# A third ring bank in PSUM, with the stick-breaking totals moved into a spent score bank

## The chip, the cores and the metric

The kernel runs on one core of one Trainium2 chip. The metric is device microseconds from the start to the end of one launch. Five engines work side by side and meet only at semaphores: TensorE (PE: matmuls, its weight loads are shown as PEld), VectorE (DVE), ScalarE (ACT), GpSimd (POOL) and SyncE (SP, which issues most DMAs). PE writes to PSUM alone, which has eight banks of 128 partitions x 512 float32 columns. All eight are in use here.

## The reference, cut to what matters

Two layers of a hybrid decoder. Each normalises x, projects it once for three branches (retention, stick-breaking attention, a conformer convolution), gates each branch, and projects the result back. What the change touches is the stick-breaking attention:

```
z = jnp.einsum('bqhd,bkhd->bhqk', qb, kb).astype(jnp.float32) * scale + bf
log_stop = jnp.where(mask, jax.nn.log_sigmoid(-z), 0.0)
after = lax.cumsum(log_stop, axis=3, reverse=True) - log_stop
A = jnp.where(mask, jnp.exp(jax.nn.log_sigmoid(z) + after), 0.0)
outs.append(jnp.einsum('bhqk,bkhd->bqhd', A.astype(v.dtype), vb))
```

The sum over later keys runs over all keys, so a kernel that goes through the keys block by block has to carry, for each query, the total of `log_stop` of the block that it has just done: what was gathered before is scaled by `exp(-total)`.

## The kernel before

1024 prompt tokens and 32 sampled ones stand as 1056 columns, in three chunks of 352 (`CH`, `CW`). A layer goes over three pairs of heads, p = 0, 1, 2. The order of all work is one list, `STEPS`, made once; every engine walks the same list and does its own part of each step, in that order, so an engine's queue is in the order of the list.

**Ring jobs.** Projections (`proj`: 24 matmuls for a chunk, in two float32r parts each, L691 to L693), rotations (`rot`), value transposes (`vtok`), the retention's steps (`att`, `ro`, `ds9`) and the norms' means and variances (`gn_...`, `ln_...`, `pw`) each write one PSUM bank of a ring of two, in turn. A job is drained by ACT or DVE. `claim` makes PE wait, ahead of a job, until the job two before it has been drained:

```
if jobs[job] >= 2:
    pe.wait_ge(*drained(in_order[jobs[job] - 2]))
```

**Stick-breaking units.** Twelve units a pair (`UNITS`): a key block `kb` against 128 to 512 queries, and two heads (h = 0, 1). Unit u has two score banks, Z[2(u%2)] and Z[2(u%2)+1]. Its steps:

- `score` (p, u): PE writes the scores into the two banks (L801, and a mask at L807). ACT takes exp (L962) into `stop`, POOL clamps it (L1484).
- ACT takes ln (L970) in step `weigh` (u-1), and DVE finishes the softplus (L1168).
- `stop` (p, u): PE adds the running sums to the scores in the banks (L814). ACT takes exp (L1122), the weights: the score bank's content is then spent. For every unit with kb > 0 (ten of twelve) PE also sums `stop` over the keys into a bank of its own, TOT (L822), for both heads, and ACT makes `keep` = exp(-total) from it (L1127).
- `weigh` (p, u): PE multiplies the weights with the values into the bank AV (L836). DVE multiplies what was gathered before by `keep` (L1380) and adds AV (L1382).

The list stands as score 0, then for each u: score u+1, stop u, weigh u. Between these the function `between` places ring jobs as filler, by fixed weights. In the first stretch of pair 1 DVE also does the convolution's taps (L1279, L1280).

The eight banks: ring0, ring1, Z0 to Z3, TOT, AV.

Of the kernel before, what the change touches and what calls it, by code (L numbers as in the profile page):

```python
# [247 lines left out]
def build(nc, io, counts):  # L248
# [4 lines left out]
    with ctx:  # L253
# [64 lines left out]
        old_x = attend[:, 0:KB * NT].rearrange("p (k n) -> p k n", k=KB)  # L318
        glu9 = sb("glu9", [P, CB, DEC_BATCH, HIST + DEC_SEQ])

        ring = [bank("ring0"), bank("ring1")]
        Z = [bank(f"Z{i}") for i in range(4)]
        TOT, AV = bank("TOT"), bank("AV")

        SUM_X, SUM_Y = [z[:, 0:CW] for z in Z[:3]], [z[:, 0:CW] for z in (Z[3], TOT, AV)]

        def cc(a, n=P):
            return const[:, a:a + n]
# [16 lines left out]
        U, B = len(UNITS), len(BLOCKS)  # L345

        z9 = Z[0][:, 0:6 * NS]

        def of_head(a, h):

# [160 lines left out]
        in_order = list(jobs)  # L511

        def in_ring(job):
            return ring[jobs[job] % 2][:, 0:CW]

        def bank_of(job):
            return ring[jobs[job] % 2]


        def scores_of(p, n, w):  # L520
# [147 lines left out]
        def _(pe):  # L668
            def claim(job):

                if jobs[job] >= 2:
                    pe.wait_ge(*drained(in_order[jobs[job] - 2]))

            for step in STEPS:
                kind = step[0]
# [25 lines left out]
                elif kind == "vtok":  # L701
# [3 lines left out]
                        pe.wait_ge(s_copy.sem, s_copy.at(job_of(name, p, CH - 1)))  # L705
                    for n in range(3 * j, 3 * j + 3):
                        t0 = n * P if n < QB else LAST
                        last = nc.tensor.transpose(ring[jobs[step] % 2][:, (n - 3 * j) * P:(n - 3 * j + 1) * P],
                                                   v_rows[:, t0:t0 + P], ident)
                    last.then_inc(s_full.sem, s_full.mark(step))  # L710
                elif kind == "att":
# [74 lines left out]
                elif kind == "score":  # L786
# [5 lines left out]
                    elif u == 0:  # L792
# [4 lines left out]
                            pe.wait_ge(s_masks, 16)  # L797
                        pe.wait_ge(s_copy.sem, s_copy.at(job_of("sk", p, CH - 1)))
                    for h in range(2):
                        r = slice(64 * h, 64 * h + 64)  # L800
                        last = nc.tensor.matmul(Z[2 * (u % 2) + h][:, 0:n], sb_k[r, kb * P:(kb + 1) * P], sb_q[r, q0:q0 + n],  # L801
                                                start=True, stop=not diagonal, skip_group_check=True)
                        if not diagonal:
                            last.then_inc(s_z.sem, s_z.mark((p, u, h)))
# [4 lines left out]
                elif kind == "stop":  # L809
                    p, u = step[1:]  # L810
                    kb, q0, n = UNITS[u]
                    for h in range(2):
                        pe.wait_ge(s_sp.sem, s_sp.at((p, u, h)))
                        nc.tensor.matmul(Z[2 * (u % 2) + h][:, 0:n], negtri, stop[:, (2 * u + h) % 4, 0:n], start=False,  # L814
                                         stop=True, skip_group_check=True).then_inc(s_za.sem, s_za.mark((p, u, h)))
                    if kb > 0:
                        if UNITS[u - 1][0] > 0:
                            pe.wait_ge(s_keepf.sem, s_keepf.at((p, u - 1)))
                        elif p > 0:
                            pe.wait_ge(s_keepf.sem, s_keepf.at((p - 1, U - 1)))  # L820
                        for h in range(2):
                            last = nc.tensor.matmul(TOT[64 * h:64 * h + 64, 0:n], ones[:, 0:64], stop[:, (2 * u + h) % 4, 0:n],  # L822
                                                    start=True, stop=True, skip_group_check=True)
                        last.then_inc(s_tot.sem, s_tot.mark((p, u)))
                elif kind == "weigh":
                    p, u = step[1:]
                    kb, q0, n = UNITS[u]
                    if u == 0:
                        pe.wait_ge(s_copy.sem, s_copy.at(("vtok", "sv", p, CH - 1)))
                        if p > 0:  # L830
                            pe.wait_ge(s_o.sem, s_o.at((p - 1, "sample")))
                    else:
                        pe.wait_ge(s_o.sem, s_o.at((p, u - 1)))
                    for h in range(2):
                        pe.wait_ge(s_a.sem, s_a.at((p, u, h)))
                        last = nc.tensor.matmul(AV[64 * h:64 * h + 64, 0:n], sb_v[:, kb, 64 * h:64 * h + 64],  # L836
                                                weight[:, h, 0:n], start=True, stop=True, skip_group_check=True)
                    last.then_inc(s_av.sem, s_av.mark((p, u)))
                elif kind == "sample_z":
                    p = step[1]  # L840
                    w = 2 * NS
                    zs = z9.rearrange("p (g b n) -> p g b n", g=3, b=DEC_BATCH)
                    q9 = q9_pad[:].rearrange("p h (b t) -> p b h t", b=DEC_BATCH)
                    pe.wait_ge(s_a.sem, s_a.at((p, U - 1, 1)))
                    pe.wait_ge(s_pagek.sem, s_pagek.at(p))
                    nc.tensor.matmul(z9[:, 2 * w:3 * w], sb_k[:, LAST:NT], q9, start=True, stop=False, skip_group_check=True)
                    nc.tensor.matmul(z9[:, 2 * w:3 * w], ident_b[:], masks[:, P:P + w], start=False, stop=False, skip_group_check=True)
                    for b in range(DEC_BATCH):
                        for g in range(N_PAGES):
                            last = nc.tensor.matmul(zs[:, g, b], page[:, b * N_PAGES + g, :], q9[:, b], start=False,  # L850
                                                    stop=False, skip_group_check=True)
                    last.then_inc(s_z.sem, s_z.mark((p, "sample")))
                elif kind == "sample_t":
                    p = step[1]
                    w = 2 * NS
                    pe.wait_ge(s_sp.sem, s_sp.at((p, "sample")))
                    s9 = stop9[:].rearrange("p g n -> p (g n)")

                    nc.tensor.matmul(z9, negtri, s9, start=False, stop=False, skip_group_check=True)
                    nc.tensor.matmul(z9[:, 0:2 * w], negones, s9[:, w:3 * w], start=False, stop=False, skip_group_check=True)  # L860
                    nc.tensor.matmul(z9[:, 0:w], negones, s9[:, 2 * w:3 * w], start=False, stop=True,
                                     skip_group_check=True).then_inc(s_za.sem, s_za.mark((p, "sample")))
                elif kind == "sample_v":
                    p = step[1]
                    w = 2 * NS
                    pe.wait_ge(s_a.sem, s_a.at((p, "sample")))
                    pe.wait_ge(s_pagev.sem, s_pagev.at(p))
                    pe.wait_ge(s_o.sem, s_o.at((p, U - 1)))
                    nc.tensor.matmul(AV[:, 0:w], sb_v[:, QB, :], weight9[:, 2, :], start=True, stop=False, skip_group_check=True)
                    for b in range(DEC_BATCH):  # L870
                        for g in range(N_PAGES):
                            q = slice(b * 2 * DEC_SEQ, (b + 1) * 2 * DEC_SEQ)
                            last = nc.tensor.matmul(AV[:, q], page[:, b * N_PAGES + g, :], weight9[:, g, q],
                                                    start=False, stop=(b == DEC_BATCH - 1 and g == N_PAGES - 1), skip_group_check=True)
                    last.then_inc(s_av.sem, s_av.mark((p, "sample")))
                elif kind == "sum_x":
                    c = step[1]
                    for k in range(KB):
                        pe.wait_ge(s_sqa.sem, s_sqa.at(("x", c, k)))
                        nc.tensor.matmul(SUM_X[c], ones, square_of_x(c, k), start=(k == 0), stop=(k == KB - 1)).then_inc(  # L880
                            s_sqm.sem, s_sqm.mark((c, k)))

        @block.scalar
        def _(act):
# [88 lines left out]
            for step in STEPS:  # L973
# [79 lines left out]
                elif kind == "vtok":  # L1053
                    _, name, p, j = step
                    if p > 0 and j == 0:
                        if name == "rv":
                            act.wait_ge(s_ds.sem, s_ds.at((p - 1, QB, 1)))
                        else:
# [1 line left out]
                    to = ret_v if name == "rv" else sb_v  # L1060
                    act.wait_ge(s_full.sem, s_full.at(step))
                    nc.scalar.activation(to[:, 3 * j:3 * j + 3, :],
                                         ring[jobs[step] % 2][:, 0:3 * P].rearrange("p (n e) -> p n e", n=3),
                                         ACT.Copy).then_inc(s_copy.sem, s_copy.mark(step))
                elif kind == "att":
                    p, n = step[1:]
# [46 lines left out]
                elif kind == "stop":  # L1113
# [6 lines left out]
                    for h in range(2):  # L1120
                        act.wait_ge(s_za.sem, s_za.at((p, u, h)))
                        nc.scalar.activation(weight[:, h, 0:n], Z[2 * (u % 2) + h][:, 0:n], ACT.Exp,  # L1122
                                             bias=vv(V_BIAS + 2 * p + h)).then_inc(s_a.sem, s_a.mark((p, u, h)))
                    if kb > 0:
                        act.wait_ge(s_tot.sem, s_tot.at((p, u)))
                        act.wait_ge(s_o.sem, s_o.at((p, u - 1)))
                        nc.scalar.activation(keep[:, 0:n], TOT[:, 0:n], ACT.Exp, scale=-1.0).then_inc(  # L1127
                            s_keepf.sem, s_keepf.mark((p, u)))
                elif kind == "weigh":
                    p, u = step[1:]  # L1130
                    if u + 1 < U:
                        ln_scores(p, u + 1)
                elif kind in ("sample_z", "sample_t"):
                    p = step[1]
                    name, to, ready, done = ("e", stop9, s_z, s_e) if kind == "sample_z" else ("a", weight9, s_za, s_a)
# [456 lines left out]
```

## Time and profile before

| | |
|---|---|
| median of 3 runs | 1669.7 us (1668.9 to 1672.17) |
| the profiled execution's own time | 1669.24 us |
| its span, first to last instruction | 1667.6 us |
| PE busy | 1531.7 us, 92% of the span |
| DVE, ACT, POOL busy | 736.2, 686.7, 582.8 us |
| mean granted clock of TensorE | 0.950 of full |

A row of a timeline gives the start and the length of an instruction or of a run of like ones, engine, line of the code, what it writes and reads, and in brackets how long the engine had been idle before it and who ended that. A matmul's row is longer than the distance to the next matmul, since matmuls are pipelined. A float32 matmul stands as two records.

### The profile page before, as it was taken

What the parts mean: (1) busy time and instruction counts of PE and PEld (TensorE: products, weight loads), DVE (VectorE), ACT (ScalarE), POOL (GpSimd) and SP (SyncE); (2) the same over time, 40 slices, a digit from 0 to 9 for tenths busy, and PEclk for the clock granted to TensorE, in tenths of its full rate; (3) what the DMA queues carried; (4) which work ended last, traced back from release to release, by engine and by line L of the source; (5) the groups of instructions that cost most, each with busy time, mean ns of one, the idle gap of its engine ahead of it and who ended that gap; (6) DMA issues with size and microseconds to landing.
All of it is one profiled execution on the core that took longest, in us unless ns stands there. A gap on an engine that the chain in (4) does not pass through costs nothing. (4 is left out here: it accounts for less than half of the span.)

```text
span 1667.6 us, 22298 instructions
## 1 busy us (share of the span) xinstructions
PE 1531.7 (92%) x8356; PEld 1229.3 (74%) x8356; DVE 736.2 (44%) x1175; ACT 686.7 (41%) x1339; POOL 582.8 (35%) x471
## 2 busy tenths in 40 slices
PE   5999999999999998999759999989989999899995
PEld 3876698666796666999548767986658966669994
DVE  4232317885353333241661323179763533433417
ACT  5344512534524644443343344224444256435423
POOL 2353412545224243141443443115541242422315
PEclk8999989999999999899979999899999999998998
DMA  6400024100221000231252000231002200004213
GB/s 238 159 26 26 13 70 78 47 26 13 76 74 39 26 14 27 62 132 51 95 161 104 26 26 13 91 79 38 13 13 86 89 14 26 14 28 133 73 45 122
DMA packets 75673, 103.69 MB, mean 62 GB/s; under 512 B 14371, under 2 KB 61219, under 8 KB 75427
## 3 DMA queue, kind: packets, MB, share of 16 engines
q1 hardware_dynamic: 64176, 60.64, 11.3%
q10 hardware_dynamic: 11378, 41.53, 7.6%
q8 instruction: 68, 1.11, 0.3%
q14 instruction: 51, 0.41, 0.1%
HBM read 74.26 MB, written 27.88 MB: 61 GB/s over the span
## 5 line engine op out<-in xcount | busy, mean ns | idle before, releaser
L691 PE MATMUL ring<-H_hi,w_hi 128*128 128x352 f32 x1824 | 622.2, 341 | 19.2 <-ACT sb_k L1023 6.0
L692 PE MATMUL ring<-H_lo,w_hi 128*128 128x352 f32 x1824 | 597.6, 328 | 0.0
L693 PE MATMUL ring<-H_hi,w_lo 128*128 128x352 f32 x1824 | 597.5, 328 | 0.0
L691 PEld LDWEIGHTS ring<-H_hi,w_hi 128*128 128x128 f32 x1824 | 353.4, 194 | 74.7 <-issue 43.4
L692 PEld LDWEIGHTS ring<-H_lo,w_hi 128*128 128x128 f32 x1824 | 354.1, 194 | 4.2 <-issue 3.0
L693 PEld LDWEIGHTS ring<-H_hi,w_lo 128*128 128x128 f32 x1824 | 352.5, 193 | 0.0
L1420 POOL TENSOR_TENSOR w_lo<-w_raw,w_hi 128x1024 fp32r<-128x1024 f32 x76 | 190.9, 2512 | 364.3 <-ACT w_hi L896 364.3
L1484 POOL TENSOR_SCALAR attend<-attend 128x512 f32<-128x512 f32 (+4 forms) x144 | 178.9, 1259 | 275.3 <-ACT attend L962 275.3
L1168 DVE SCALAR_TENSOR_TENSOR attend<-Z,vec_sb,attend 128x512 f32<-128x512 f32 (+4 forms) x144 | 82.4, 611 | 219.7 <-ACT attend L970 219.6
L1279 DVE SCALAR_TENSOR_TENSOR MX<-MX,vec_sb 128x1023 f32<-128x1023 f32 (+29 forms) x120 | 156.4, 1304 | 0.1
L814 PE MATMUL Z<-attend,const 128*128 128x512 f32 (+5 forms) x288 | 108.8, 502 | 2.5 <-DVE attend L1168 2.5
L896 ACT ACTIVATE w_hi<-w_raw 128x1024 fp32r<-128x1024 f32 x76 | 80.2, 1055 | 36.2 <-PE ring L693 30.2
L1122 ACT ACTIVATE attend<-Z,vec_sb 128x512 f32<-128x512 f32 (+4 forms) x144 | 80.0, 580 | 21.9 <-PE Z L814 19.5
L1036 ACT ACTIVATE gate<-ring 128x352 f32<-128x352 f32 x54 | 25.0, 462 | 154.8 <-PE ring L693 154.8
L962 ACT ACTIVATE attend<-Z,vec_sb 128x512 f32<-128x512 f32 (+4 forms) x144 | 75.6, 577 | 27.9 <-PE Z L807 21.1
L1242 DVE TENSOR_TENSOR sb_k<-sb_k,wide 128x352 f32<-128x352 f32 x42 | 26.3, 627 | 128.5 <-ACT wide L1047 128.3
L1433 POOL TENSOR_TENSOR qd<-ret_q,decay_sb 128x256 f32<-128x256 f32 (+1 forms) x54 | 45.0, 834 | 93.0 <-PE ring L734 93.0
L814 PEld LDWEIGHTS Z<-attend,const 128*128 128x128 f32 x288 | 52.9, 196 | 31.6 <-issue 14.7
L970 ACT ACTIVATE attend<-attend 128x512 f32<-128x512 f32 (+4 forms) x144 | 68.0, 516 | 14.8 <-POOL attend L1484 14.7
L1041 ACT ACTIVATE MX<-ring 128x352 f32<-128x352 f32 x48 | 22.2, 463 | 116.2 <-PE ring L693 116.2
L836 PE MATMUL AV<-attend 128*64 128x512 f32 (+5 forms) x288 | 64.7, 520 | 3.6 <-ACT attend L1122 3.6
L801 PE MATMUL Z<-sb_q,sb_k 64*128 64x512 f32 (+5 forms) x288 | 67.8, 548 | 0.0
(149 smaller groups left out, 1779.0 us busy)
## 6 DMA issues: line engine op xcount, KB each, us to landing
w_raw<-in_w ACTq DMA_DIRECT2D x76, 512.0 KB, 3.5
out_yT<-MX SPq DMA_DIRECT2D x6, 1408.0 KB, 9.3
attend<-out_yT SPq DMA_DIRECT2D x6, 1408.0 KB, 10.1
out_yT<-MX SPq DMA_DIRECT2D x12, 704.0 KB, 3.3
attend<-in_cache_k SPq DMA_DIRECT2D x96, 64.0 KB, 1.9
attend<-in_cache_v SPq DMA_DIRECT2D x96, 64.0 KB, 1.9
MX<-in_xT SPq DMA_DIRECT2D x3, 1408.0 KB, 11.7
out_k_rows<-sb_k SPq DMA_DIRECT2D x6, 528.0 KB, 2.8
```

Source lines behind the costliest of these rows:

```text
L691: nc.tensor.matmul(in_ring(step), a, x, start=(k == 0), stop=False)
L692: nc.tensor.matmul(in_ring(step), a, y, start=False, stop=False)
L693: last = nc.tensor.matmul(in_ring(step), b, x, start=False, stop=(k == KB - 1))
L814: nc.tensor.matmul(Z[2 * (u % 2) + h][:, 0:n], negtri, stop[:, (2 * u + h) % 4, 0:n], start=False, stop=True, skip_group_check=True).then_ ...
L896: nc.scalar.activation(w_hi[:, i % 2, :], w_raw[:], ACT.Copy).then_inc(s_whi.sem, s_whi.mark(i))
L962: nc.scalar.activation(stop[:, (2 * u + h) % 4, 0:n], Z[2 * (u % 2) + h][:, 0:n], ACT.Exp, bias=vv(V_BIAS + 2 * p + h)).then_inc(s_e.sem, ...
L970: nc.scalar.activation(s, s, ACT.Ln, bias=1.0).then_inc(s_l.sem, s_l.mark((p, u, h)))
L1122: nc.scalar.activation(weight[:, h, 0:n], Z[2 * (u % 2) + h][:, 0:n], ACT.Exp, bias=vv(V_BIAS + 2 * p + h)).then_inc(s_a.sem, s_a.mark((p, ...
L1168: nc.vector.scalar_tensor_tensor(out=s, in0=Z[2 * (u % 2) + h][:, 0:n], scalar=vv(V_BIAS + 2 * p + h), in1=s, op0=ALU.add, op1=ALU.max).th ...
L1279: nc.vector.scalar_tensor_tensor(out=y, in0=glu[b][:, 0:SEQ - s], scalar=w, in1=y, op0=ALU.mult, op1=ALU.add)
L1420: nc.gpsimd.tensor_tensor(w_lo[:, i % 2, :], w_raw[:], w_hi[:, i % 2, :].bitcast(F32), ALU.subtract).then_inc(s_wlo.sem, s_wlo.mark(i))
L1484: nc.gpsimd.tensor_scalar(s, s, E_MAX, None, ALU.min).then_inc(s_min.sem, s_min.mark((p, u, h)))
```

## The change

The ring gets a third bank, and a job waits for the job three before it. The bank comes from TOT, which is gone: the totals of unit u go into the second head's score bank, Z[2(u%2)+1], once its weights have been taken. So PE's two matmuls for the totals move from `stop` to `weigh`, ahead of the value product, behind a wait for the second head's exp (`s_a`); ACT's `keep` moves from `stop` to `weigh`, behind the two ln of unit u+1; and PE's second score matmul of unit u+2 now waits for `keep` of unit u (`s_keepf`), which reads the bank that it writes. `stop` no longer waits for `keep`. The row sums at a layer's end use other banks (AV, Z1).

```
-        ring = [bank("ring0"), bank("ring1")]
+        ring = [bank("ring0"), bank("ring1"), bank("ring2")]
+        RING = len(ring)
         Z = [bank(f"Z{i}") for i in range(4)]
-        TOT, AV = bank("TOT"), bank("AV")
-        SUM_X, SUM_Y = [z[:, 0:CW] for z in Z[:3]], [z[:, 0:CW] for z in (Z[3], TOT, AV)]
+        AV = bank("AV")
+        SUM_X, SUM_Y = [z[:, 0:CW] for z in Z[:3]], [z[:, 0:CW] for z in (Z[3], AV, Z[1])]
...
+        def total_of(u):
+            return Z[2 * (u % 2) + 1][:, 0:UNITS[u][2]]
...
-                if jobs[job] >= 2:
-                    pe.wait_ge(*drained(in_order[jobs[job] - 2]))
+                if jobs[job] >= RING:
+                    pe.wait_ge(*drained(in_order[jobs[job] - RING]))
...
                     for h in range(2):
+                        if h == 1 and u >= 2 and UNITS[u - 2][0] > 0:
+                            pe.wait_ge(s_keepf.sem, s_keepf.at((p, u - 2)))
...
-                    if kb > 0:
-                        if UNITS[u - 1][0] > 0:
-                            pe.wait_ge(s_keepf.sem, s_keepf.at((p, u - 1)))
-                        elif p > 0:
-                            pe.wait_ge(s_keepf.sem, s_keepf.at((p - 1, U - 1)))
-                        for h in range(2):
-                            last = nc.tensor.matmul(TOT[64 * h:64 * h + 64, 0:n], ones[:, 0:64], stop[:, (2 * u + h) % 4, 0:n],
-                                                    start=True, stop=True, skip_group_check=True)
-                        last.then_inc(s_tot.sem, s_tot.mark((p, u)))
                 elif kind == "weigh":
...
+                    if kb > 0:
+                        pe.wait_ge(s_a.sem, s_a.at((p, u, 1)))
+                        for h in range(2):
+                            last = nc.tensor.matmul(total_of(u)[64 * h:64 * h + 64, :], ones[:, 0:64], stop[:, (2 * u + h) % 4, 0:n],
+                                                    start=True, stop=True, skip_group_check=True)
+                        last.then_inc(s_tot.sem, s_tot.mark((p, u)))
...
+                elif kind == "weigh":
+                    p, u = step[1:]
+                    kb, q0, n = UNITS[u]
+                    if u + 1 < U:
+                        ln_scores(p, u + 1)
                     if kb > 0:
                         act.wait_ge(s_tot.sem, s_tot.at((p, u)))
                         act.wait_ge(s_o.sem, s_o.at((p, u - 1)))
-                        nc.scalar.activation(keep[:, 0:n], TOT[:, 0:n], ACT.Exp, scale=-1.0).then_inc(
+                        nc.scalar.activation(keep[:, 0:n], total_of(u), ACT.Exp, scale=-1.0).then_inc(
                             s_keepf.sem, s_keepf.mark((p, u)))
-                elif kind == "weigh":
-                    p, u = step[1:]
-                    if u + 1 < U:
-                        ln_scores(p, u + 1)
```

PE's queue before, in pair 0, from behind unit 4's two stop matmuls to unit 6's scores (transposes L708 and `att` L716, L718 are filler; bank numbers are part of the names, `attend` holds `stop`, weights and values; in brackets the semaphores waited for):

```order
L822 MATMUL TOT<-attend,const 64x384 [waits s_keepf]
L822 MATMUL TOT<-attend,const 64x384
L708 MATMUL ring0<-const,attend 128x128 [waits s_copy]
L708 MATMUL ring0<-const,attend 128x128 x2
L708 MATMUL ring1<-const,attend 128x128 [waits s_copy]
L708 MATMUL ring1<-const,attend 128x128 x2
L716 MATMUL ring0<-qd,kd 128x256 [waits s_dec,s_copy]
L718 MATMUL ring0<-const,kd 128x128
L836 MATMUL AV<-attend 64x384 [waits s_a,s_o]
L836 MATMUL AV<-attend 64x384 [waits s_a]
L801 MATMUL Z0<-sb_q,sb_k 128x320 [waits s_a]
L801 MATMUL Z1<-sb_q,sb_k 128x320
```

The same place in the change (lines have moved on by a few: L712 is L708, L720 and L722 are L716 and L718, L834 the totals, L839 the value product, L807 the scores):

```order
L712 MATMUL ring1<-const,attend 128x128 [waits s_copy]
L712 MATMUL ring1<-const,attend 128x128 x2
L712 MATMUL ring2<-const,attend 128x128 [waits s_copy]
L712 MATMUL ring2<-const,attend 128x128 x2
L720 MATMUL ring0<-qd,kd 128x256 [waits s_dec,s_copy]
L722 MATMUL ring0<-const,kd 128x128
L834 MATMUL Z1<-attend,const 64x384 [waits s_a,s_o]
L834 MATMUL Z1<-attend,const 64x384
L839 MATMUL AV<-attend 64x384 [waits s_a] x2
L807 MATMUL Z0<-sb_q,sb_k 128x320 [waits s_a]
L807 MATMUL Z1<-sb_q,sb_k 128x320 [waits s_keepf]
```

The totals stand behind the filler now, directly ahead of the value product, and the second score matmul has a wait that it did not have.

ACT's queue at the same place, before (L1062 drains a transpose, L1072 the `att` step's keys; L1122 are unit 4's weights, L970 unit 5's ln, L962 unit 6's exp):

```order
L1122 ACTIVATE attend<-Z0,vec_sb 128x384 [waits s_za,s_av]
L1122 ACTIVATE attend<-Z1,vec_sb 128x384 [waits s_za]
L1127 ACTIVATE keep<-TOT 128x384 [waits s_o,s_tot]
L1062 ACTIVATE attend<-ring0 128x384 [waits s_full]
L1062 ACTIVATE attend<-ring1 128x384 [waits s_full]
L1072 ACTIVATE kd_tok<-ring0 128x128 [waits s_attm]
L970 ACTIVATE attend<-attend 128x384 [waits s_min] x2
L962 ACTIVATE attend<-Z0,vec_sb 128x320 [waits s_z,s_tot,s_za]
```

And in the change:

```order
L1125 ACTIVATE attend<-Z0,vec_sb 128x384 [waits s_za,s_av]
L1125 ACTIVATE attend<-Z1,vec_sb 128x384 [waits s_za]
L1065 ACTIVATE attend<-ring1 128x384 [waits s_full]
L1065 ACTIVATE attend<-ring2 128x384 [waits s_full]
L1075 ACTIVATE kd_tok<-ring0 128x128 [waits s_attm]
L973 ACTIVATE attend<-attend 128x384 [waits s_min] x2
L1135 ACTIVATE keep<-Z1 128x384 [waits s_o,s_tot]
L965 ACTIVATE attend<-Z0,vec_sb 128x320 [waits s_z,s_tot,s_za]
```

`keep` (L1127, now L1135) has moved behind the drains, the key copy and both ln of the next unit.

## Rows read from the trace of the kernel before

**Rows 1.** The page: span, and busy time of the engines.
```profile
span 1667.6 us, 22298 instructions
PE 1531.7 (92%) x8356; PEld 1229.3 (74%) x8356; DVE 736.2 (44%) x1175; ACT 686.7 (41%) x1339; POOL 582.8 (35%) x471
```

**Rows 2.** Groups of PE by line: busy, mean ns | idle before, who ended it.
```profile
L691 PE MATMUL ring<-H_hi,w_hi 128*128 128x352 f32 x1824 | 622.2, 341 | 19.2 <-ACT sb_k L1023 6.0 <-DVE sb_q L1199 4.6 <-ACT kd_tok L1072 2.8
...
L716 PE MATMUL ring<-qd,kd 128*128 128x256 f32 (+1 forms) x108 | 34.7, 403 | 21.4 <-POOL kd L1437 19.5 <-ACT MX L1106 1.1 <-ACT attend L1062 0.5
...
L730 PE MATMUL ring<-qd,state 128*128 128x128 f32 x168 | 27.4, 286 | 1.3 <-DVE MX L1224 1.3
...
L880 PE MATMUL Z<-attend,const 128*128 128x352 f32 x64 | 25.2, 559 | 30.1 <-ACT attend L926 30.1
...
L708 PE MATMUL ring<-const,attend 128*128 128x128 f32 x108 | 17.2, 283 | 7.1 <-ACT attend L1018 3.9 <-ACT attend L1062 1.9 <-ACT MX L1106 1.1
L763 PE MATMUL ring<-MX,const 128*128 128x352 f32 x36 | 16.0, 527 | 8.4 <-DVE MX L1224 5.7 <-DVE sb_q L1199 2.7
```

**Rows 3.** PE's waits, by who ended them: us, times, longest.
```profile
PE ring L691 <- ACT sb_k L1023: 6.0, 2, 3.0
...
PE Z L814 <- DVE attend L1168: 2.5, 2, 1.3
PE ring L691 <- POOL w_lo L1420: 1.2, 2, 0.6
...
PE ring L783 <- DVE MX L1359: 0.9, 2, 0.5
...
PE ring L716 <- ACT attend L1062: 0.5, 2, 0.3
```

**Rows 4.** Timeline of PE at the longest wait for a ring bank, pair 0.
```profile
49.13 0.32 PE L692 MATMUL ring<-H_lo,w_hi 128*128 128x352 f32 x1
49.29 0.32 PE L693 MATMUL ring<-H_hi,w_lo 128*128 128x352 f32 x1
52.60 0.43 PE L691 MATMUL ring<-H_hi,w_hi 128*128 128x352 f32 x1 [2.99 <-ACT sb_k L1023]
```

**Rows 5.** Timeline of DVE and PE at the start of pair 1.
```profile
257.98 0.86 PE L763 MATMUL ring<-MX,const 128*128 128x352 f32 x2 [1.31 <-DVE sb_q L1199]
...
261.13 0.66 PE L691 MATMUL ring<-H_hi,w_hi 128*128 128x352 f32 x1 [2.29 <-DVE sb_q L1199]
...
267.68 0.52 DVE L1199 TENSOR_SCALAR sb_q<-ring 128x352 f32<-128x352 f32 x1 [4.83 <-PE ring L693]
...
282.02 0.53 DVE L1335 TENSOR_TENSOR MX<-MX,rstd 128x352 f32<-128x352 f32 x1 [2.57 <-ACT rstd L906]
```

**Rows 6.** Stretches: length, busy PE, PEld, DVE, ACT, POOL; clock, DMA.
```profile
259.60:266.50 6.90, 5.37 (x18) 5.37 (x19) 3.25 (x6) 0.50 (x1) 0.00 (x0) 0.51 1.18 82
...
665.80:669.20 3.40, 2.99 (x6) 1.85 (x6) 1.31 (x3) 1.35 (x3) 0.21 (x1) 0.50 0.00 0
```

**Rows 7.** Timeline of PE at pair 2's second group mean.
```profile
666.21 1.54 PE L763 MATMUL ring<-MX,const 128*128 128x352 f32 x2 [2.84 <-DVE MX L1224]
```

**Rows 8.** Timeline of ACT and PE around unit 4's value product, pair 0.
```profile
140.64 0.49 ACT L1127 ACTIVATE keep<-TOT 128x384 f32<-128x384 f32 x1 [0.22 <-PE TOT L822]
142.96 0.28 ACT L1072 ACTIVATE kd_tok<-ring 128x128 f32<-128x128 f32 x1 [0.98 <-DVE att L1294]
143.13 0.93 ACT L970 ACTIVATE attend<-attend 128x384 f32<-128x384 f32 x2
...
142.39 0.87 PE L836 MATMUL AV<-attend 128*64 128x384 f32 x4
143.19 0.81 PE L801 MATMUL Z<-sb_q,sb_k 64*128 64x320 f32 x4
```

**Rows 9.** Timeline of PE in pair 1: totals, and a late weight.
```profile
363.05 0.87 PE L822 MATMUL TOT<-attend,const 128*64 128x384 f32 x4
...
420.82 1.24 PE L836 MATMUL AV<-attend 128*64 128x384 f32 x4 [1.79 <-ACT attend L1122]
```

More of the change, by code:

```diff
@@ L513, in in_ring @@
         def in_ring(job):
-            return ring[jobs[job] % 2][:, 0:CW]
+            return ring[jobs[job] % RING][:, 0:CW]
         def bank_of(job):
-            return ring[jobs[job] % 2]
+            return ring[jobs[job] % RING]
         def scores_of(p, n, w):
@@ L707, in _ @@
                         t0 = n * P if n < QB else LAST
-                        last = nc.tensor.transpose(ring[jobs[step] % 2][:, (n - 3 * j) * P:(n - 3 * j + 1) * P],
+                        last = nc.tensor.transpose(ring[jobs[step] % RING][:, (n - 3 * j) * P:(n - 3 * j + 1) * P],
                                                    v_rows[:, t0:t0 + P], ident)
@@ L1062, in _ @@
                     nc.scalar.activation(to[:, 3 * j:3 * j + 3, :],
-                                         ring[jobs[step] % 2][:, 0:3 * P].rearrange("p (n e) -> p n e", n=3),
+                                         ring[jobs[step] % RING][:, 0:3 * P].rearrange("p (n e) -> p n e", n=3),
                                          ACT.Copy).then_inc(s_copy.sem, s_copy.mark(step))
```

## The prediction

> **What bounds the kernel now.** I read the page first: PE is busy for 1531.7 of 1667.6 us [rows 1], so it is the engine to look at, and what can be had without less work are the 136 us in which it stands idle. The second view splits this idle time by the line of PE that stood and by who let it go [rows 2]. The reader is to sort it in two. On one side stand waits for data: 30.1 us for the first squares of a layer (L880), 19.5 us of the retention's decayed keys from POOL (L716), 3.9 us for copied values (L708). On the other side stand waits for a ring bank: the one who ends them is a drain of the job two before. To these belong L691's 19.2 us without 1.2 us that end with a weight split [rows 3], so 18.0; 1.6 of L716 (both ACT releasers); 1.3 of L730; 3.0 of L708 (its last two releasers); 8.4 of L763. Sum: 32.3 us. In the list of waits these are thirteen rows with 36 waits; the first and the last stand in [rows 3].
>
> The third view, a timeline, shows that such a wait costs a little more than its idle time [rows 4]: a projection matmul's row is 0.32 us long, but the next one starts 0.16 us after it, so 0.16 us of every wait lie hidden under the last row. It shows the mechanism too: the second `sk` chunk at 52.60 stands 2.99 us until ACT has copied the first, while the bank of the job before that is long empty.
>
> The stick-breaking chain itself (exp, clamp, ln, softplus, exp) hardly stops PE: 2.5 us at the stop matmuls (L814) [rows 3], because ring jobs fill its latency.
>
> **The change part by part.** *Third bank.* Every one of the 36 bank waits would now be for the drain of the job three before. At each of them I compared when that older drain was done with when PE was ready: it was done in all. So the whole 32.3 us go, and 36 x 0.16 = 5.8 us with them: **38.1 us** for both layers. Three corrections follow.
>
> First, pair 1's start [rows 5]. Each layer has three bank waits in a row here, because DVE does convolution taps between its drains: 1.31, 2.29 and 0.3 us, about 4.4 us with the hidden parts. The granted clock is 0.51 from 259.60 to 266.50 [rows 6], the lower level (1.2 GHz), and in the 3.1 us ahead of 261.13 PE had stood idle for 1.31 and 2.29 us. With three banks the last `sq` chunk waits for the drain that let PE go at 257.98, and no longer for the one at 261.13. Its 24 matmuls then take 24 x 0.16 = 3.9 us at full clock and end near 261.9. DVE, which stood 4.83 us until that chunk's end (267.68), can drain it when it is free at 262.85. So PE gains 5.6 to 6 us here and DVE 4.83, and part of its next idle time (2.57 at 282.02, which ends with work that PE's earlier start brings forward). I take 5.9 us a layer, 1.5 above the waits: **+3.0** for both layers. Bounds: DVE's 4.83 below, PE's waits and half the slow stretch (4.4 + 3.4 = 7.8) above.
>
> Second, what is eaten by a later wait for data. The transposes of pair 1's values wait some 0.7 us a layer for banks, but behind them stands the first stop matmul, which waits for DVE's softplus (L814) [rows 3]: 1.4 us lost. In pair 2 the bank wait behind a rotation (0.6 us) stands ahead of the pointwise product's wait for the convolution's norm (L783, 0.9 in two) [rows 3]: 1.3 lost; and of the value transposes between those products I count 0.7 as lost, since two drains stand behind one another there. Together **-3.4**. Bounds: nothing, or half of the sum.
>
> Third, the group mean of pair 2 [rows 7]. The 2.84 us go, but the projection behind it waits for the same late drain at 666.2; against that stands a slow stretch (clock 0.50 from 665.80 to 669.20 [rows 6], PE idle for 2.84 ahead of it), of which part should go. I set one against the other: 0.
>
> *The totals moved.* PE does the same 240 records as before; four of them are 0.87 us (L822) [rows 9]. A move costs PE only where the totals filled a wait and no longer do. In pair 1 there are four such places a layer: three `att` steps that wait for POOL (of the 19.5 us of [rows 2]), and unit 9, where PE already waits 1.79 us for the weights [rows 9]: at each the 0.6 us that the totals take net of overlap now come behind the wait. At three places in the same pair the totals move into a wait behind the value product, and give 0.6 back. Net 0.6 a layer, **-1.2**. Bounds: 0, and all four places unpaid with 0.87 us, -7.0.
>
> *The new wait of the second score matmul.* Behind it in PE's queue stand the mask matmuls and the next projection, and ACT's exp waits for those scores. It is due where little filler stands between `weigh` u and `score` u+2. The tightest place is unit 4 [rows 8]: value product at 142.39, scores at 143.19, the second head's some 0.4 later, so 1.2 us after `weigh` began; with the totals ahead of the product, 1.8. On ACT the key copy (142.96) and two ln (143.13, 0.93 us) come first, so `keep` can start at 144.06, which is 1.67 behind the beginning, and takes 0.49 (140.64): 2.16. The wait is 0.4 us. At the next two places with 1.3 us between product and second score, only a projection's drain and the ln stand ahead of `keep`, and it comes within 0.1 us of being in time; elsewhere more filler hides it, a whole projection (3.9 us) or more at half of the scores. **-0.8** for both layers. Bounds: 0, and one `keep` length (0.49) at each of the 48 scores, 23.5. I stay near the lower end, as the tightest place gives 0.4.
>
> DVE's product with `keep` does not come later for it: it stands behind unit u+1's softplus, which needs the same two ln. The other edits (row sums into other banks, `stop` without its wait) touch no wait that shows.
>
> Sum: 38.1 + 3.0 - 3.4 - 1.2 - 0.8 = 35.7 us. The profiled execution took 1669.2 in all (span 1667.6); less 35.7 this is 1633.5. The median of the runs is 0.5 above the profiled one, so I predict **1634 us**.
>
> A rule of the Trainium skill bears on the clock term. The row says: clock 0.51 for 6.9 us and 0.50 for 3.4 us behind waits for a bank [rows 6]. "TensorE: Matmul & The Clock Gate", section "A second HAM failure mode: psum-queue depth-cycling", tells of a kernel whose PE idles briefly between groups as it cycles through banks, so that the clock goes up and down and the cost is paid between bursts. By that, both stretches would go with the waits, at half their length each (3.4 + 1.7 a layer, 10.2 in all) in place of my 3.0; the trace agrees in that these stretches follow such waits.
>
> **The rivals.**
>
> *Given back (1650 us).* A bank wait only shows that ACT or DVE is late; PE, set free, runs into the next wait on the same engine. For it speaks the pattern at the transposes, where it happened in my own count. Then what stays are the waits behind which the late engine catches up: the `sk` chunk (6.0 + 0.3), pair 2's mean (5.7 + 0.3) and pair 1's start (8.8), 21.1, less 2.0 for the new waits: 19, or 1650. Against it: the later waits of the rest are for work that itself follows PE, so it moves with it.
>
> *More (1623 us).* Both slow stretches vanish (+7.2 over my 3.0) and nothing is eaten (+3.4): 1634 - 10.6. Against it: DVE is nearly the bound at pair 1's start.
>
> *Keep is late (1676 us, slower).* ACT serves its queue in order; `keep` now stands behind drains and ln, and PE stands behind `keep` at 48 scores. If each waits 0.9 us in place of a mean of 0.02, 42 us are lost: 1676. It decides from 35.7/48 = 0.74 us a score. For it speaks that ACT's ln come 1.67 us behind the beginning of `weigh`; against it, that a projection of 3.9 us stands ahead of every second score.
>
> *No gain (1671 us).* PE's idle time is data's, and deeper banks change nothing. For it speaks that more idle time is for data than for banks in [rows 2]; against it each bank row's releaser. Time: 1669.7 plus the new waits' 2.0, 1671.7, and a little back. The Trainium skill has a case of this kind ("TensorE: Matmul & The Clock Gate", section "HAM oscillation — how this bites in real kernels"): adding PSUM double buffering to a kernel already rearranged gave no further gain. The trace does not agree, by the 18.0 us of L691.
>
> **How the numbers follow.** Chances: forecast (1625 to 1643) 0.60, given back 0.18, more 0.12, no gain 0.05, late keep 0.05. Leaving out the last two and the outer edges of the second and third, the range is 1622 to 1652. About 0.2% (3.3 us) is what a measurement of this kernel tells from no change. Faster by more than that: 0.60 + 0.18 + 0.12 = 0.90; within: 0.05; slower: 0.05.
>
> **What would show it.** Of PE's idle time the bank releasers (`sk`, `sq`, key copy, rotation, gates) should be down from 32.3 to under 5 us, with data waits as before. Pair 1's start should show no idle time of DVE near 4.8 us. The second score matmul should show `keep` as releaser for less than 2 us in all, the totals ACT's exp for 2 to 4 us in unit 9. The prediction is wrong if the time stays and the idle time of PE only changes its releasers, or if `keep` ends waits of PE for over 10 us.

## The result, and the profile after

The changed kernel takes 1617.95 us in the median (1613.06 to 1624.49, 4 runs), the kernel before beside it 1670.93 (1668.9 to 1679.72, 4 runs): a ratio of 0.9676, 95% interval 0.9626 to 0.9725. That is 53 us less where 36 were predicted, and 4 us below the range. The profiled execution took 1618.99 us. One run of e1 below, 1761.25 us at a mean clock of 0.814 where its others have 0.946 to 0.949, is left out of its ratio and its products.

The page after, to be held against [rows 1]: span, and busy time of the engines.

```profile
span 1617.3 us, 22296 instructions
PE 1502.3 (93%) x8356; PEld 1235.4 (76%) x8356; DVE 735.5 (45%) x1175; ACT 681.5 (42%) x1339; POOL 579.3 (36%) x471
```

The span is 50.3 us shorter. PE's idle time, span less busy, fell from 135.9 to 115.0, by 20.9; the other 29.4 us came off its *busy* time, although it runs the same 8356 matmul records. The clock did not do that: its mean is 0.947 in this execution, and was 0.950. Of PE's busy time the forecast touched only the 5.8 us of hidden tails, so some 24 us of the fall stood in none of its terms.

PE's waits after, by who ended them (us, times, longest), to be held against [rows 2, 3]:

```profile
PE Z L883 <- ACT attend L929: 31.2, 2, 21.5
PE ring L720 <- POOL kd L1441: 25.3, 16, 3.7
...
PE Z L834 <- ACT attend L1125: 7.0, 4, 3.3
PE ring L712 <- ACT attend L1021: 3.9, 6, 0.6
...
PE Z L820 <- DVE attend L1172: 3.2, 2, 1.6
...
PE ring L695 <- DVE sb_q L1203: 1.7, 2, 0.8
PE ring L695 <- POOL w_lo L1424: 1.2, 2, 0.6
...
PE ring L767 <- ACT attend L1065: 0.6, 2, 0.3
PE ring L712 <- ACT MX L1109: 0.5, 2, 0.2
```

The bank waits are gone as forecast: of 32.3 us stay 2.8 (the `sq` drain's 1.7, 0.6 at the group mean, 0.5 at the transposes). Waits for data grew: POOL's keys by 5.8 (L716 before, L720 now), the totals' wait for ACT's exp stands at 7.0 where the value product waited 3.6. No row names `keep` as the end of a wait of a score matmul.

Where the busy time went, PE's timeline shows around unit 4's totals. Before:

```profile
138.34 1.46 PE L814 MATMUL Z<-attend,const 128*128 128x384 f32 x4
139.73 0.87 PE L822 MATMUL TOT<-attend,const 128*64 128x384 f32 x4
140.53 0.87 PE L708 MATMUL ring<-const,attend 128*128 128x128 f32 x6
...
142.39 0.87 PE L836 MATMUL AV<-attend 128*64 128x384 f32 x4
143.19 0.54 PE L801 MATMUL Z<-sb_q,sb_k 64*128 64x320 f32 x2
```

After:

```profile
144.00 0.87 PE L834 MATMUL Z<-attend,const 128*64 128x384 f32 x4
144.67 0.84 PE L839 MATMUL AV<-attend 128*64 128x384 f32 x4
145.45 0.43 PE L695 MATMUL ring<-H_hi,w_hi 128*128 128x352 f32 x1
145.71 0.32 PE L696 MATMUL ring<-H_lo,w_hi 128*128 128x352 f32 x1
```

The shape in the middle of a row is the one to read: totals and value product are 128\*64, one half of the array for each head, side by side; their neighbours are 128\*128, or 64\*128 where scores (L801) stand next. From start to next start each took 0.80 us before (139.73 to 140.53, 142.39 to 143.19); together they take 1.45 now (144.00 to 145.45), 0.15 less than 1.60. Entering costs as well: the fourth stop matmul's distance to the totals is 1.39 - 3 x 0.32 = 0.43, where its likes stand 0.32 apart; and the projection behind the value product stands 0.26 ahead of its next, where 0.16 is usual. So one visit to the half arrays fewer is worth 0.15 + 0.11 + 0.10 = 0.36 us here, an estimate from one place. The weight loads (PEld) show how it comes about. Before:

```profile
139.73 0.20 PEld L822 LDWEIGHTS TOT<-attend,const 128*64 128x64 f32 x4 [0.55 <-issue]
140.52 0.42 PEld L708 LDWEIGHTS ring<-const,attend 128*128 128x128 f32 x4 [0.60 <-issue]
```

A weight load commonly begins under the matmul ahead of it (that of L696 above at 145.55, its matmul at 145.71); at both ends of the visit it begins only with its own matmul (139.73, 140.52), 0.55 and 0.60 us after the load before it ended. The Trainium skill has one line that fits ("TensorEngine Tiling (Array Packing)", section "Key Properties"): changing the tiling mode drains TensorE. It gives no price; the trace agrees, with the 0.36 us above for in and out. In the whole program such visits (start times of all PE rows, by shape) fell from 180 to 122: 58, since two of the 60 had a 128\*64 neighbour already. The prediction did not count them.

### The profile page after: what moved, and what is told of

Same layout as the page of the kernel before. It is cut to its first block and busy times, and to the rows that moved or that the text cites. A ratio compares the mean times of both kernels' runs of the same rounds, so it can differ in the third digit from the quotient of the medians.

```text
span 1617.3 us, 22296 instructions
## 1 busy us (share of the span) xinstructions
PE 1502.3 (93%) x8356; PEld 1235.4 (76%) x8356; DVE 735.5 (45%) x1175; ACT 681.5 (42%) x1339; POOL 579.3 (36%) x471
## 5 line engine op out<-in xcount | busy, mean ns | idle before, releaser
L696 PE MATMUL ring<-H_lo,w_hi 128*128 128x352 f32 x1824 | 594.7, 326 | 0.0
L695 PEld LDWEIGHTS ring<-H_hi,w_hi 128*128 128x128 f32 x1824 | 351.1, 192 | 39.8 <-issue 32.3
L696 PEld LDWEIGHTS ring<-H_lo,w_hi 128*128 128x128 f32 x1824 | 351.9, 193 | 8.2 <-issue 5.1
L1283 DVE SCALAR_TENSOR_TENSOR MX<-MX,vec_sb 128x1023 f32<-128x1023 f32 (+29 forms) x120 | 160.2, 1335 | 0.1
L1125 ACT ACTIVATE attend<-Z,vec_sb 128x512 f32<-128x512 f32 (+4 forms) x144 | 79.9, 580 | 23.6 <-PE Z L820 21.3
L807 PE MATMUL Z<-sb_q,sb_k 64*128 64x512 f32 (+5 forms) x288 | 68.1, 535 | 0.0
L1461 POOL TENSOR_TENSOR rot_a<-raw_rot,turn_sb 128x352 f32<-128x352 f32 x36 | 36.1, 1003 | 83.7 <-ACT raw_rot L1014 83.7
```

What stands on the lines that cost most here:

```text
L695: nc.tensor.matmul(in_ring(step), a, x, start=(k == 0), stop=False)
L696: nc.tensor.matmul(in_ring(step), a, y, start=False, stop=False)
L1283: nc.vector.scalar_tensor_tensor(out=y, in0=glu[b][:, 0:SEQ - s], scalar=w, in1=y, op0=ALU.mult, op1=ALU.add)
```

## The experiments

The theory: each visit to 128\*64 tiles costs some 0.3 us (0.30 in the expectations), and totals beside the value product save one in nearly each of 60 units (*tile theory*). Rivals: the third bank gave everything (*ring theory*), or ACT's new order did, with `keep` behind the two ln (*keep theory*).

A product helps to read small steps: span times mean granted clock, run by run. The slow stretches run at half clock (0.50 to 0.51 in [rows 6]), so span x (1 - clock) is about what they cost, and the product is about the time without them. It is a rough measure: where PE stands idle in a slow stretch, as for 2.5 of 7.0 us at 346 us in the changed kernel, the first figure is more than the stretch costs, and the clock is known to three digits, which is 0.8 us either way. The product's standard deviation over the runs of one kernel is 0.5 to 2.6 us; e2's times, 14 us apart, lie within 5 by it. Means over the runs:

| kernel | ratio to before, 95% | span x clock | span x (1 - clock) |
|---|---|---|---|
| before (on four occasions) | 1 | 1584.2 to 1585.2 | 87.7 to 90.7 |
| changed, first runs | 0.9676 (0.9626 to 0.9725) | 1533.0 | 83.7 |
| changed, again (e8) | 0.9675 (0.9651 to 0.9698) | 1534.0 | 83.0 |
| e1 move, two banks | 0.9863 (0.9839 to 0.9886) | 1564.9 | 86.3 |
| e2 keep late alone | 0.9929 (0.9903 to 0.9955) | 1580.7 | 81.2 |
| e3 full-width between | 0.9876 (0.9852 to 0.9900) | 1559.1 | 95.1 |
| e4 half-width between | 0.9673 (0.9652 to 0.9693) | 1540.0 | 79.3 |
| e5 move, own bank | 0.9812 (0.9787 to 0.9837) | 1560.4 | 84.2 |
| e6 keep first | 0.9681 (0.9656 to 0.9707) | 1533.3 | 89.5 |
| e7 readouts merged | 0.9639 (0.9610 to 0.9667) | 1532.2 | 83.5 |
| e9 first head's bank | 0.9666 (0.9638 to 0.9694) | 1533.0 | 83.8 |
| e10 20 readouts merged | 0.9659 (0.9632 to 0.9685) | 1533.3 | 81.3 |
| e11 e9 and e10 | 0.9648 (0.9625 to 0.9671) | 1532.0 | 80.9 |
| e12 merged in two pairs | 0.9658 (0.9631 to 0.9684) | 1531.0 | 84.7 |

**e1, the move without the third bank.**

```
-        RING = len(ring)
+        RING = 2
```

> The changed kernel with only two of its three ring banks in use: the totals moved, no third bank. Tile theory (each visit of TensorE to its two 64-column halves costs some 0.30 us of entering and leaving, and totals beside the value product save one visit in each of 60 units): 18 us less than before, less 3.4 us of new waits for ACT's exp, so about 1656 us (1650 to 1660). Ring theory (the third bank alone gave the 50 us, the move nothing): 1669 to 1673. Keep theory (the gain beyond the ring's comes from ACT, which now does the two ln ahead of keep): about 1655 too; the kernel with keep alone moved tells it from the tile theory.

0.9863, 1653.56 us in the median: the ring theory falls. The bank waits are nearly all there still, 29.5 us of 32.3 in the wait list of this kernel, from which these rows are:

```profile
PE ring L720 <- POOL kd L1441: 21.3, 14, 3.7
...
PE Z L834 <- ACT attend L1125: 7.0, 4, 3.3
PE ring L695 <- ACT sb_k L1026: 6.0, 2, 3.0
PE ring L695 <- DVE sb_q L1203: 4.6, 2, 2.3
...
PE ring L720 <- ACT kd_tok L1075: 4.4, 2, 2.2
```

So the third bank, from here to the changed kernel, is worth 31 us by the product (1564.9 to 1533.0 and 1534.0) or by the ratios (1.88% of 1675).

**e2, `keep` late alone.** In the kernel before, ACT's block for `keep` goes from `stop` to `weigh`, behind `ln_scores(p, u + 1)`; nothing else.

> The kernel before with one edit: ACT does keep behind the two ln of the next unit, as in the changed kernel; totals, banks and PE's order stay. Tile theory and ring theory: no change, 1668 to 1673. Keep theory: about 15 us less, 1655.

0.9929: between the theories. Of the 11 us by which the median falls, the product shows 4.4. Most of them stand in its wait list:

```profile
PE ring L716 <- POOL kd L1438: 19.8, 16, 2.1
...
PE ring L763 <- DVE MX L1225: 2.0, 2, 1.0
```

The group mean's wait for DVE's gate (L763 <- DVE MX) was 5.7 us in [rows 2]. It is one of the bank waits, which the third bank ends anyway; by e6, keep's place makes no difference to the product with three banks. The rest is less slow clock, 81.2 against 89.5: its runs go from 1656.9 at a mean clock of 0.956 to 1671.3 at 0.946. Why the clock fares better here stays open.

**e3 and e4, the price of a visit.** Between totals and value product stands a needless matmul of 64 columns, full-width in e3 (the first edit), as two halves in e4 (the second); its result is overwritten.

```
+                    if kb > 0:
+                        nc.tensor.matmul(AV[:, 0:64], negtri, stop[:, (2 * u) % 4, 0:64], start=True, stop=True,
+                                         skip_group_check=True)
```

```
+                    if kb > 0:
+                        for h in range(2):
+                            nc.tensor.matmul(AV[64 * h:64 * h + 64, 0:64], ones[:, 0:64], stop[:, (2 * u + h) % 4, 0:64],
+                                             start=True, stop=True, skip_group_check=True)
```

> The changed kernel with one needless 128x128 matmul of 64 columns between the totals and the value product of each of the 60 units (its result is overwritten). Its own two records are at most 0.11 us each by the rows of 128 columns (start to start), 7 to 13 us in all. Tile theory: the full-width matmul brings the second visit back, 18 us and its own 7 to 13, so 25 to 31 us more than the changed kernel, about 1646. Ring theory and keep theory: its own 7 to 13 us alone, 1625 to 1631.

> The control to the needless full-width matmul: at the same place two needless 64-column matmuls, one for each half of the array, side by side as the totals are. All theories: its own 7 to 13 us, 1625 to 1631. If it costs as much as the full-width one, the tile theory falls, since then what lies between counts and not its width.

The control costs nothing that its ratio shows (0.9673; 6 us in the product, where 7 to 13 were expected), the full-width one 2% (0.9876: 34 us over the changed kernel, where 25 to 31 were expected). By the product e3 stands 19.1 us over e4: 60 visits at **0.32 us**, if the two needless pieces are equally long themselves. No run separates that: the halves take 0.12 us (below), and the expectation put the full-width records at 0.11 each at most, which would leave 0.22. e3's timeline of PE at unit 4, and its weight loads:

```profile
145.52 0.86 PE L834 MATMUL Z<-attend,const 128*64 128x384 f32 x4
146.31 0.44 PE L838 MATMUL AV<-attend,const 128*128 128x64 f32 x2
146.68 0.54 PE L842 MATMUL AV<-attend 128*64 128x384 f32 x2
...
146.31 0.30 PEld L838 LDWEIGHTS AV<-attend,const 128*128 128x128 f32 x2 [0.60 <-issue]
...
147.47 0.19 PEld L695 LDWEIGHTS ring<-H_hi,w_hi 128*128 128x128 f32 x1 [0.60 <-issue]
```

and e4's:

```profile
144.78 0.87 PE L834 MATMUL Z<-attend,const 128*64 128x384 f32 x4
145.44 0.31 PE L839 MATMUL AV<-attend,const 128*64 128x64 f32 x4
145.56 0.85 PE L843 MATMUL AV<-attend 128*64 128x384 f32 x4
146.34 0.43 PE L695 MATMUL ring<-H_hi,w_hi 128*128 128x352 f32 x1
```

The same 64 columns take 0.12 us from start to next start as halves (145.44 to 145.56) and 0.37 full-width (146.31 to 146.68), and the totals ahead of them 0.66 and 0.79. From the totals to the projection behind the value product it is 1.56 in e4 (144.78 to 146.34) and 1.95 in e3 (145.52 to 147.47, where the projection's weight load begins). The rest of what e3 takes over e4 is slow clock, 95.1 against 79.3; no run says why.

**e5, the move with the totals' own bank.** e2, and the block of the totals moved as it stands (TOT, its wait for `keep`) from `stop` to `weigh`, ahead of the value product.

> The kernel before with two edits: keep behind the two ln (as in the second experiment) and the totals issued directly ahead of the value product, still in their own bank, with two ring banks and without the new wait of the second score matmul. Tile theory: the visits saved are those of the first experiment, so the same ratio to before as there, 0.984 to 0.989, some 1653; the score bank does nothing of its own. If what the first experiment gained was keep's order, this run stays at the second one's 0.993, some 1664; if it was the spent score bank, too.

0.9812, better than expected. From e2 to e5 the product falls by **20.3 us**, 0.35 for each of 58 visits: the neighbourhood alone, with old banks. It came off PE's busy time (1523.5 us of a span of 1656.8 in e2's profile, 1510.0 of 1644.9 in e5's); the idle time stayed, 133.3 and 134.9. From e5 to e1 it rises by **4.5**: the price of the spent score bank. e5's wait at this place is the value product's, the last of these rows:

```profile
PE ring L716 <- POOL kd L1438: 20.6, 14, 3.7
...
PE ring L716 <- ACT kd_tok L1072: 4.4, 2, 2.2
...
PE AV L836 <- ACT attend L1122: 3.8, 2, 1.9
```

In e1 it is the totals' 7.0: they need the second head's exp, as it is its bank. That is 3.2 of the 4.5, as far as a longer wait shows as time; e9 tries it.

**e6, `keep` ahead of the two ln** in the changed kernel (the two blocks in ACT's `weigh` change places).

> The changed kernel with keep ahead of the two ln on ACT, the order of before; three banks, totals beside the value product. Tile theory: within 4 us of the changed kernel (ratio 0.966 to 0.970). Keep theory, sized by the second experiment's 0.7%: 8 to 12 us slower than the changed kernel (0.972 to 0.975).

The same as the changed kernel, 0.9681 and 1533.3. With three banks no effect of `keep`'s place shows: the keep theory falls.

**e7, more neighbours.** On PE alone, totals and value product go beside the retention readout's own 128\*64 matmuls (L738) where a weigh step stands near one:

```
+                if a[0] == "ro" and b[0] == "weigh":
+                    order += [("ro_state",) + a[1:], ("ro_values",) + a[1:], b, ("ro_add",) + a[1:]]
...
+                elif a[0] == "weigh" and b[0] == "ro":
+                    order += [("ro_state",) + b[1:], a, ("ro_values",) + b[1:], ("ro_add",) + b[1:]]
...
+                elif a[0] == "weigh" and b[0] in ("att", "taps") and c[0] == "ro":
+                    order += [b, ("ro_state",) + c[1:], a, ("ro_values",) + c[1:], ("ro_add",) + c[1:]]
...
```

> The changed kernel, and on TensorE alone at 26 places (13 a layer) where a weigh step stands beside a retention readout, totals and value product are issued directly ahead of or behind that readout's own pair of 64-column matmuls. The same matmuls, banks and waits. Tile theory: 26 visits of some 0.30 us fewer, 8 us less than the changed kernel, about 1610 (ratio 0.961 to 0.965). Without it: no change, or 1 to 3 us slower, since totals or readout come up to 1.4 us later at these places (0.968 to 0.970).

Visits fell from 122 to 100, 22 where 26 were expected, and the product by 1 to 2 us, not 8. PE's waits for the state, 0.9 us in the changed kernel, grew to 3.6; probably because the state's increment stands behind the value product in the first branch:

```profile
PE ring L760 <- DVE state L1340: 2.5, 2, 1.2
...
PE ring L752 <- DVE state L1340: 1.1, 2, 0.6
```

**e8 to e11.** e8 is the changed kernel again; e10 is e7 without its third branch; e11 is e9 and e10 together. e9:

```
-            return Z[2 * (u % 2) + 1][:, 0:UNITS[u][2]]
+            return Z[2 * (u % 2)][:, 0:UNITS[u][2]]
...
-                        if h == 1 and u >= 2 and UNITS[u - 2][0] > 0:
+                        if h == 0 and u >= 2 and UNITS[u - 2][0] > 0:
...
-                        pe.wait_ge(s_a.sem, s_a.at((p, u, 1)))
+                        pe.wait_ge(s_a.sem, s_a.at((p, u, 0)))
```

> The changed kernel once more, unchanged, beside the next three on one chip. All theories: ratio 0.966 to 0.970; span times granted clock (the time with its slow stretches taken out) 1532 to 1534, as in its first runs, which would say that differences of 2 us in this product can be read.

> The changed kernel with the totals in the spent score bank of the first head; the first score matmul of unit u+2 waits for keep in place of the second. If the spent bank's cost (4.5 us between the fifth and the first experiment, in span times clock) is the wait for the second head's exp, PE's wait at the totals falls from 7.0 to about 3.8 us and span times clock by 3 us, to 1530. If the cost lies elsewhere, no change; if keep now comes late for the first head's score, slower by up to 5 us.

> The seventh experiment without its six places at which a retention score step was drawn ahead of the totals: 20 places where weigh and readout stand directly beside one another. Tile theory with the seventh experiment's lesson (the waits for the state ate what the visits gave): the visits saved stay some 17, the waits grow less, span times clock 1529 to 1532. If the visits beside a readout are worth nothing, 1533.

> The ninth and the tenth edit together on the changed kernel, the candidate for the fastest: the sum of the two, span times clock about 1527, 6 us under the changed kernel; 1533 if neither edit gives anything.

e8 agrees with the first runs. e9 gives nothing that can be told (1533.0, where 1530 was hoped for): its totals wait less, but the first score matmul now waits for `keep`.

```profile
PE Z L834 <- ACT attend L1125: 5.6, 2, 2.8
...
PE Z L807 <- ACT keep L1135: 2.4, 6, 0.7
```

e10 misses (1533.3; the same 3.6 us of waits for the state as e7), e11 is 2 us below the changed kernel in the product, less than was hoped.

**e12, e7 in pairs 0 and 2 alone** (its conditions with `a[1] != 1`).

> The seventh experiment with its edit in pairs 0 and 2 alone, 18 of the 26 places. In its trace, set against that of the changed kernel at the ends of projections and with the slow stretches taken out, these two pairs gained 3.7 us over both layers and pair 1 lost 2.3, where PE's waits for the state grew. If that reading is right: PE's waits for DVE's state stay near 0.9 us, and span times clock is 3.7 us under the changed kernel's 1533.5, about 1530 (1529 to 1531), the fastest of all. If the visits beside a readout are worth nothing: 1533 to 1534.

PE's waits for the state are back at 0.9 us, and the product is 1531.0, the lowest: some 2.5 under the changed kernel, for 16 visits fewer (106), where 3.7 were expected. As the lowest of five tries it may owe part of that to chance. By its ratio it can't be told from the changed kernel, nor can e7 or e11. No version is shown to beat it in time.

## Why the prediction was wrong

**The step that failed is "The totals moved".** It said that "PE does the same 240 records as before" and that a move "costs PE only where the totals filled a wait": -1.2 us, with bounds of 0 and -7.0. Its best bound was 0, so no gain could come out of it, and none of the rivals had one. Measured, the move is worth +20.3 for the neighbourhood (e5 against e2; e3 against e4 gives 19.1 by another way) and -4.5 for the spent bank (e1 against e5), **+15.8** together. With the wait of the second score matmul (-0.8 forecast, no such wait in the profile) the forecast had -2.0 here: 17.8 us too little, about the miss (53 less 36). The cost that the step did name came as well: the waits at the keys (L716) rose from 19.8 us in e2 to 25.0 in e5 (20.6 for POOL, 4.4 for a drain); the 20.3 are net of it. The evidence stood in the trace of before: in [rows 9] four records of totals last 0.87 us, and the step itself priced them at 0.6 "net of overlap", but did not ask what the two ends of the group cost.

**Third bank: right, and near in size.** Forecast were 38.1 + 3.0 - 3.4 = 37.7 us. Measured are 31 from e1 to the changed kernel, and the 4.4 of e2, counted here because most of them come from the same wait list: 35.4 in span x clock, which leaves out what the clock gave.

**Pair 1's start: right.** The changed kernel's stretches (length; busy PE, PEld, DVE, ACT, POOL with counts; clock, DMA):

```profile
248.00:262.00 14.00, 14.00 (x87) 13.79 (x86) 13.92 (x21) 2.87 (x5) 2.41 (x1) 1.00 0.50 58
346.00:353.00 7.00, 4.50 (x12) 2.23 (x14) 4.68 (x8) 1.44 (x5) 3.76 (x5) 0.52 0.00 0
```

Clock 1.00, the higher of the two levels (2.4 GHz), where pair 1 starts now and [rows 6] had 0.51; DVE works through, and its 4.83 us of [rows 5] are gone. At pair 2's second group mean, where [rows 6] had 0.50 and the forecast set gain against loss, the clock is 1.00 as well (642 to 650 us), and PE works through. But slow stretches came elsewhere: the second row, at the lower level, begins within PE's 3.7 us wait for POOL's keys, the longest of this kind, which was 2.1 before; it is 3.7 in e1 and e5 too, so it came with the move. In all, span x (1 - clock) went from 87.7 to 83.0 us where e8 ran, 4.7. By the rule that the prediction quoted from the Trainium skill ("TensorE: Matmul & The Clock Gate", section "A second HAM failure mode: psum-queue depth-cycling"), 10.2 were to go; the trace agrees with it at the two places that it was applied to, and not in the sum.

**Eaten by later waits: near in sum by luck.** From e1 to the changed kernel POOL's keys took 4.0 us more (21.3 and 25.3) and softplus 0.6 (2.6 and 3.2), 4.6 against 3.4. But the forecast had 1.4 at softplus, 1.3 at the pointwise product, whose 0.9 us of waiting are gone (L783, now L787), and 0.7 at transposes; the keys stood in none of these terms. There a wait for a drain, 4.4 us in e1 and absent before, became a wait for POOL: 25.7 in e1 for both, 25.3 now. That data waits would stay as before was wrong: they grew, mostly with the move. The totals' wait in unit 9, forecast at 2 to 4 us, is 3.3.

**Rivals.** *Given back* and *no gain* fall with the 31 us from e1 to the changed kernel, *late keep* with the wait list. *More* came closest in time, but not by its reason: the two slow stretches went, others came, and all the clock gave is 4.7 us.

## What to carry to other kernels

When a matmul moves, look at the tile shape of its old and new neighbours, not only at its own length: price a group from its start to the next start, in and out, and count the changes of shape before and after. Here a weight load that began only with its own matmul marked such a change. The bank waits that the third bank removed were worth about what the wait list said, less what the next waits for data took back.

## What was not expected of the hardware

A visit to 128\*64 tiles cost 0.35 us (e5 against e2) in and out, by the other way 0.32 (e3 against e4, or 0.22 at the least). Beside a readout of 128 columns it was worth only 0.16 (2.5 us for 16 visits in e12); that is at the limit of what the product can tell, and why is not settled. And needless visits brought more slow clock with them (95.1 us in e3, 79.3 in e4), though PE was busy for 93% of the span in both; that stays open too.
